# A triangular inverse by levels: the products of levels 1 to 4 on diagonal blocks of 32 instead of 64

## The chip, the cores and the metric

The kernel runs on one core of a Trainium2 chip. The metric is the device time of one execution in microseconds, as the median of several executions. One execution was also recorded by the hardware profiler; its rows are what this document argues from.

## The reference

The program is a stack of two models over 256 tokens of width 1024 in float32, with feed-forward blocks, several token mixers and norms. Two of its mixers are gated delta rules with 8 heads of width 128, worked in chunks of 64 tokens. For each chunk and head a lower triangular system is solved:

```python
CHUNK = 64
GDN_HEADS = 8

def gated_delta_rule(q, k, v, g, beta):
    ...
    a_mat = jnp.where(strict, jnp.einsum('nbhid,nbhjd->nbhij', kb, kc) * decay, 0.0)
    t_mat = a_mat + jnp.eye(CHUNK, dtype=jnp.float32)
    rhs = jnp.concatenate([vc * bc[..., None], kb * jnp.exp(gc)[..., None]], axis=-1)
    sol = lax.linalg.triangular_solve(t_mat, rhs, left_side=True, lower=True, unit_diagonal=True)
    value, kcd = sol[..., :dv], sol[..., dv:]
    ...
```

The matrix `t_mat` is 64x64, with ones on its diagonal. There are 4 chunks and 8 heads in each mixer, 32 such systems.

## The kernel before

The kernel writes out the program of each engine by hand, and semaphores connect them. All weights come through one stream of chunks of 1 MB: SyncE loads a chunk, ACT makes its rounded part `w_hi` (`split_high`, L395), DVE the rest `w_lo` (`split_low`, L402), and PE multiplies with three matmuls for each pair of 128x128 tiles (L408 to L410). A gated-delta mixer goes through its input chunks in steps `u`. In step `u` PE runs `before(u)`, the first half of the product with chunk `u`, `middle(u)`, and the second half. The small products of the delta rule are put in `before` and `middle`.

The kernel inverts the triangular matrices instead of solving. A pair of chunks is held at once, one on partitions 0 to 63 and one on 64 to 127; `t` (0 or 1) counts the pairs, and `h` the 8 heads. `g_A` holds the matrix below the diagonal, `g_T` and `g_TT` the inverse so far and its transpose. Level 0 makes the inverses of the 2x2 blocks on the diagonal, and level `v` joins blocks of 2^v rows into blocks of 2^(v+1), up to level 5, which joins two of 32 (`LEVELS` is 6). A level takes three products and two steps on DVE:

- `right(v)` on PE (in `middle`): the product of `g_A` and `g_T` into PSUM bank `4 + t`. DVE multiplies it by the mask of the level into `g_Y` (`right_set`, L2904); the mask has ones in only those entries that this level fills.
- `both(v)` on PE (in `before` of the next step): `g_TT` with `g_Y` into bank `4 + t` (not at level 5), and `g_Y` with `g_TT` into bank `6 + t`. DVE subtracts whole banks from `g_T` (L2910) and from `g_TT` (L2911), in `inverse_set`.

Each product is made by `blocks`, whose 16 matmuls are 64 rows by 64 columns on the two diagonal 64x64 tiles of the array:

```python
        def blocks(bank, lhs, rhs):

            for h in range(HN):
                for r in CK:
                    last = nc.tensor.matmul(ps[r, bank, CHUNK * h:CHUNK * h + CHUNK], lhs[r, h, :], rhs(r, h), start=True, stop=True)
            return last
```

All these operands are float32 and not its rounded form, and a matmul of theirs is two records of weight load and two of matmul in the trace. `right(1)` is in `middle(10)`, `both(1)` in `before(11)`, and so on to `right(5)` in `middle(14)` and `both(5)` in `before(15)`. Between them DVE also works on the convolution (L2844), the scaled values (L2921) and `w_lo`.

Of the kernel before, what the change touches and what calls it, by code (L numbers as in the profile page):

```python
# [24 lines left out]
CHUNK = 64  # L25
# [157 lines left out]
LEVELS = 6  # L183
# [63 lines left out]
def two_block_model(nc, w, out):  # L247

    plan, start = weight_plan(w)
# [34 lines left out]
    ps = ctx.enter_context(nc.psum_tensor("ps", [P, 8, 512], F32))  # L284
# [546 lines left out]
    def cols(k, a, b, rows=slice(0, P)):  # L831
        return ws[k][rows, a:b]
# [21 lines left out]
    blocks = cols(5, 800, 1760).rearrange("p (v j n) -> p v j n", v=2, n=2 * N_CMP)  # L854
# [840 lines left out]
    HN = 8  # L1695
# [97 lines left out]
    def mixer_tensor(pe, i, xpass_out, edge):  # L1793
        (gdn_tensor, mlstm_tensor, diff_tensor)[i % 3](pe, i, xpass_out, edge)
# [521 lines left out]
    def by_block(k, part):  # L2316
        return ws[k][:, D * part:D * part + D].rearrange("p (t h c) -> p t h c", t=TT, c=CHUNK)

    def chunk_tmp(e):
        return ws[9][:, D + 512 * (e % 2):D + 512 * (e % 2) + 512].rearrange("p (a s) -> p a s", a=2)  # L2320
# [3 lines left out]
    g_dec, g_A, g_T, g_TT, g_Y = by_block(6, 0), by_block(6, 1), by_block(7, 0), by_block(7, 1), by_block(9, 0)  # L2324
# [33 lines left out]
    inv_y, inv_ys, inv_z, inv_t = (gp("inverse_right", TT * LEVELS), gp("inverse_right_set", TT * (LEVELS - 1)),  # L2358
                                   gp("inverse_both", TT * (LEVELS - 1)), gp("inverse_set", TT * LEVELS))
# [56 lines left out]
    def gdn_tensor(pe, i, xpass, edge):  # L2416
# [4 lines left out]
# [6 lines that stand above are left out]
# [43 lines left out]
        def turned_chunk(bank, src):  # L2470

            for t in range(TT):
                for a in range(2):
                    last = nc.tensor.transpose(ps[:, bank, (2 * t + a) * P:(2 * t + a + 1) * P], src[:, a, t * P:(t + 1) * P], ident)
            last.then_inc(gd_tn.sem, 1)
# [6 lines left out]
        def v_turned(c):  # L2482
# [4 lines left out]
                done(gd_ssx, 0)  # L2487
            turned_chunk(3, chunk_tmp(c))

        def right(v):  # L2490
            for t in range(TT):
                if v == 1:
                    done(gd_T0, t)
                else:
                    done(inv_t, TT * (v - 1) + t)
                blocks(4 + t, g_A[:, t, :, :], lambda r, h: g_T[r, t, h, :]).then_inc(inv_y.sem, 1)

        def both(v):
            for t in range(TT):
                done(inv_ys, TT * (v - 1) + t)  # L2500
                if v < LEVELS - 1:
                    blocks(4 + t, g_TT[:, t, :, :], lambda r, h: g_Y[r, t, h, :])
                blocks(6 + t, g_Y[:, t, :, :], lambda r, h: g_TT[r, t, h, :]).then_inc(inv_z.sem, 1)

        def values_reads(t):
            done(inv_t, TT * (LEVELS - 1) + t)
# [59 lines left out]
        def before(u):  # L2566
# [24 lines left out]
            if 11 <= u <= 15:  # L2591
                both(u - 10)
# [8 lines left out]
        def middle(u):  # L2601
            if u == 8:
                for t in range(TT):
                    if t == 0:
                        done(gd_kc, 1)
                    token_products(4 + t, g_kT, g_kT, t).then_inc(gd_kk.sem, 1)
            if 10 <= u <= 14:
                right(u - 9)
            if u == 15:
                values_reads(0)  # L2610
            if u == 16:
                done(gd_z, 2)
                attention(1)
                first_gain()
# [8 lines left out]
        for u in range(3, 17):  # L2623
# [5 lines left out]
            bank = (u - 1) % 3  # L2629
# [596 lines left out]
```

## Time and profile before

| what | value |
|---|---|
| median of 3 runs | 2469.0 us (2468.1 to 2474.7) |
| the profiled execution | 2470.6 us |
| its span, first to last instruction | 2468.8 us |
| PE, matmuls | 2403.3 us busy, 97% of the span |
| PEld, weight loads | 2222.7 us, 90% |
| DVE | 1501.5 us, 61% |
| ACT | 1068.1 us, 43% |
| POOL | 151.8 us, 6% |
| granted TensorE clock, mean | 0.993 |

PE is the matmul side of TensorE and PEld its weight loads, which overlap. The ends of matmuls are modelled, and records overlap, so the busy time of a group is the time that its records cover together, and the spacing of their starts says more than the length of one. A shape `64*64 64x128` is 64 rows by 64 weight columns, with 64 rows of 128 moving columns.

### The profile page before, as it was taken

How to read it: one execution, taken by the hardware profiler on the slowest of the kernel's cores; microseconds unless marked ns; L12 is line 12 of the kernel's file. 1: busy time of each engine (PE TensorE's matmuls, PEld its weight loads, DVE VectorE, ACT ScalarE, POOL GpSimd, SP SyncE). 2: the span in 40 equal slices, each digit the busy share in tenths (PEclk: the TensorE clock that was granted, in tenths of full speed). 3: DMA queues.
4: the chain of work that ended last, by engine and by line, in shares of the span. 5: the costliest groups of instructions: out<-in, count | busy, mean ns of one | idle time of the engine just before them, and what ended most of it. 6: DMA issues, size and time to landing. Idle time of an engine off the chain costs nothing. (4 is left out here: it accounts for less than half of the span.)

```text
span 2468.8 us, 42893 instructions
## 1 busy us (share of the span) xinstructions
PE 2403.3 (97%) x18882; PEld 2222.7 (90%) x18882; DVE 1501.5 (61%) x2042; ACT 1068.1 (43%) x1319; POOL 151.8 (6%) x177
## 2 busy tenths in 40 slices
PE   8999999999999999999999999999998999999998
PEld 8999889999999799899889989899997998998997
DVE  5457664465567645667565556755676556866554
ACT  4334643333336543363343345533465335533432
POOL 0100000020000100001110000100001000111000
PEclk9999999999999999999999999999999999999999
DMA  6756355575564455543155554555545555423553
GB/s 228 241 188 155 107 175 184 186 226 190 185 165 128 151 187 186 158 139 104 53 196 188 188 156 137 171 188 188 178 137 171 188 188 162 121 87 103 181 188 118
DMA packets 320809, 405.37 MB, mean 164 GB/s; under 512 B 48688, under 2 KB 281232, under 8 KB 320624
## 3 DMA queue, kind: packets, MB, share of 16 engines
q1 hardware_dynamic: 314960, 383.50, 49.1%
q0 software_dynamic: 5664, 19.13, 2.5%
q8 instruction: 149, 2.44, 0.4%
q14 instruction: 36, 0.29, 0.0%
HBM read 401.55 MB, written 1.05 MB: 163 GB/s over the span
## 5 line engine op out<-in xcount | busy, mean ns | idle before, releaser
L402 DVE TENSOR_TENSOR w_lo<-raw,w_hi 128x2048 fp32r<-128x2048 f32 (+2 forms) x363 | 813.6, 2266 | 123.7 <-ACT w_hi L395 123.4
L395 ACT CAST w_hi<-raw 128x2048 fp32r<-128x2048 f32 (+2 forms) x363 | 685.5, 1890 | 462.5 <-PE ps L410 403.8
L408 PE MATMUL ps<-aT_hi,w_hi 128*128 128x256 f32 x2840 | 810.3, 285 | 0.0
L409 PE MATMUL ps<-aT_lo,w_hi 128*128 128x256 f32 x2840 | 804.4, 283 | 0.0
L410 PE MATMUL ps<-aT_hi,w_lo 128*128 128x256 f32 x2840 | 804.3, 283 | 0.0
L408 PEld LDWEIGHTS ps<-aT_hi,w_hi 128*128 128x128 f32 x2840 | 543.3, 191 | 7.0 <-issue 1.9
L409 PEld LDWEIGHTS ps<-aT_lo,w_hi 128*128 128x128 f32 x2840 | 543.5, 191 | 4.2 <-issue 0.5
L410 PEld LDWEIGHTS ps<-aT_hi,w_lo 128*128 128x128 f32 x2840 | 543.3, 191 | 0.5
L408 PE MATMUL ps<-w_hi,h_hi 128*128 128x512 f32 x928 | 363.6, 392 | 5.8 <-DVE h_lo L1758 4.6
L409 PE MATMUL ps<-w_lo,h_hi 128*128 128x512 f32 x928 | 362.6, 391 | 0.0
L410 PE MATMUL ps<-w_hi,h_lo 128*128 128x512 f32 x928 | 361.4, 389 | 0.0
L408 PE MATMUL ps<-w_hi,aT_hi 128*128 128x256 f32 (+2 forms) x992 | 303.7, 306 | 18.0 <-DVE aT_lo L732 14.4
L409 PE MATMUL ps<-w_lo,aT_hi 128*128 128x256 f32 (+2 forms) x992 | 297.1, 299 | 0.0
L410 PE MATMUL ps<-w_hi,aT_lo 128*128 128x256 f32 (+2 forms) x992 | 297.0, 299 | 0.0
L408 PEld LDWEIGHTS ps<-w_hi,aT_hi 128*128 128x128 f32 x992 | 191.6, 193 | 29.2 <-DVE aT_lo L732 17.5
L408 PEld LDWEIGHTS ps<-w_hi,h_hi 128*128 128x128 f32 x928 | 174.8, 188 | 40.8 <-DVE h_lo L1758 6.0
L410 PEld LDWEIGHTS ps<-w_hi,h_lo 128*128 128x128 f32 x928 | 174.5, 188 | 37.1
L409 PEld LDWEIGHTS ps<-w_lo,h_hi 128*128 128x128 f32 x928 | 174.9, 188 | 32.6
L593 DVE TENSOR_TENSOR ws<-ws 128x512 f32<-128x512 f32 x64 | 44.2, 691 | 262.1 <-ACT ws L686 262.1
L410 PEld LDWEIGHTS ps<-w_hi,aT_lo 128*128 128x128 f32 x992 | 191.8, 193 | 5.8
L409 PEld LDWEIGHTS ps<-w_lo,aT_hi 128*128 128x128 f32 x992 | 191.9, 193 | 5.2
L593 DVE TENSOR_TENSOR ws<-ws,ps 128x512 f32<-128x512 f32 x44 | 30.2, 687 | 258.4 <-PE ps L410 258.4
(370 smaller groups left out, 1944.6 us busy)
## 6 DMA issues: line engine op xcount, KB each, us to landing
raw<-in_mlp_w SPq DMA_DIRECT2D x128, 1024.0 KB, 5.4
raw<-in_ffn_wd SPq DMA_DIRECT2D x44, 1024.0 KB, 4.9
raw<-in_ffn_wg SPq DMA_DIRECT2D x43, 1024.0 KB, 5.3
raw<-in_ffn_wu SPq DMA_DIRECT2D x43, 1024.0 KB, 5.3
raw<-in_gdn_w_in SPq DMA_DIRECT2D x32, 1024.0 KB, 5.7
raw<-in_mlstm_w_in SPq DMA_DIRECT2D x12, 1024.0 KB, 5.4
raw<-in_diff_w_in SPq DMA_DIRECT2D x12, 1024.0 KB, 5.3
raw<-in_w_in SPq DMA_DIRECT2D x8, 1024.0 KB, 5.2
```

Of the source, the lines that this page charges most:

```text
L395: nc.scalar.copy(used_part(hi_slot(n), n), used_part(raw[:, n % RAW, :], n)).then_inc(hi_ready, 1)
L402: nc.vector.tensor_tensor(used_part(lo_slot(n), n), used_part(raw[:, n % RAW, :], n), used_part(hi_slot(n), n).bitcast(F32), ALU.subtract) ...
L408: nc.tensor.matmul(dst, l_hi, r_hi, start=start, stop=False)
L409: nc.tensor.matmul(dst, l_hi, r_lo, start=False, stop=False)
L410: return nc.tensor.matmul(dst, l_lo, r_hi, start=False, stop=stop)
L593: nc.vector.tensor_tensor(hidden_buffer(s), gate, up, ALU.mult).then_inc(hid_made, 1)
```

## The change

A new function `blocks_of_32` makes a product for the levels 1 to 4: for each head, four matmuls of 32 rows and 32 weight columns, one on each of the four diagonal 32x32 tiles of the array, which `tile_position` names. Everything off these diagonal blocks is left out. At these levels the mask has no entry there, and `g_T` and `g_TT` are zero there. Since DVE still subtracts whole banks, the bank must hold zeros off the blocks: in `both(1)` the product into bank `6 + t` therefore takes all 64 moving columns (`zeros_too`), and the later levels leave these entries as they are. Bank `4 + t` holds zeros there since the product with the identity in `before(10)`, which `blocks` still makes whole. Level 5 and all work on DVE and ACT stay as they were.

```diff
--- before.py
+++ after.py
@@ -2487,20 +2487,37 @@
                 done(gd_ssx, 0)
             turned_chunk(3, chunk_tmp(c))
 
+        def blocks_of_32(bank, lhs, rhs, zeros_too=False):
+
+            for h in range(HN):
+                for q in range(4):
+                    r, own = slice(32 * q, 32 * q + 32), slice(32 * (q % 2), 32 * (q % 2) + 32)
+                    c = slice(0, CHUNK) if zeros_too else own
+                    last = nc.tensor.matmul(ps[r, bank, CHUNK * h + c.start:CHUNK * h + c.stop], lhs[r, h, own], rhs[r, h, c],
+                                            start=True, stop=True, tile_position=(32 * q, 32 * q))
+            return last
+
         def right(v):
             for t in range(TT):
                 if v == 1:
                     done(gd_T0, t)
                 else:
                     done(inv_t, TT * (v - 1) + t)
-                blocks(4 + t, g_A[:, t, :, :], lambda r, h: g_T[r, t, h, :]).then_inc(inv_y.sem, 1)
+                if v < LEVELS - 1:
+                    last = blocks_of_32(4 + t, g_A[:, t, :, :], g_T[:, t, :, :])
+                else:
+                    last = blocks(4 + t, g_A[:, t, :, :], lambda r, h: g_T[r, t, h, :])
+                last.then_inc(inv_y.sem, 1)
 
         def both(v):
             for t in range(TT):
                 done(inv_ys, TT * (v - 1) + t)
                 if v < LEVELS - 1:
-                    blocks(4 + t, g_TT[:, t, :, :], lambda r, h: g_Y[r, t, h, :])
-                blocks(6 + t, g_Y[:, t, :, :], lambda r, h: g_TT[r, t, h, :]).then_inc(inv_z.sem, 1)
+                    blocks_of_32(4 + t, g_TT[:, t, :, :], g_Y[:, t, :, :])
+                    last = blocks_of_32(6 + t, g_Y[:, t, :, :], g_TT[:, t, :, :], v == 1)
+                else:
+                    last = blocks(6 + t, g_Y[:, t, :, :], lambda r, h: g_TT[r, t, h, :])
+                last.then_inc(inv_z.sem, 1)
 
         def values_reads(t):
             done(inv_t, TT * (LEVELS - 1) + t)
```

What PE now has in place is seen from the order of its instructions in the built program; `x64` is the count of equal matmuls one after the other. First, the start of step 11 in the first mixer, where `before(11)` stands between the product of chunk 10 and that of chunk 11. Before:

```order
L408 MATMUL ps<-aT_hi,w_hi 128x256
L409 MATMUL ps<-aT_lo,w_hi 128x256
L410 MATMUL ps<-aT_hi,w_lo 128x256
L2425 MATMUL ps<-ws 64x64 x64
L2474 MATMUL ps<-consts,ws 128x128 x4
L408 MATMUL ps<-aT_hi,w_hi 128x256
L409 MATMUL ps<-aT_lo,w_hi 128x256
L410 MATMUL ps<-aT_hi,w_lo 128x256
```

and with the change:

```order
L408 MATMUL ps<-aT_hi,w_hi 128x256
L409 MATMUL ps<-aT_lo,w_hi 128x256
L410 MATMUL ps<-aT_hi,w_lo 128x256
L2496 MATMUL ps<-ws 32x32 x32
L2496 MATMUL ps<-ws 32x64 x32
L2496 MATMUL ps<-ws 32x32 x32
L2496 MATMUL ps<-ws 32x64 x32
L2474 MATMUL ps<-consts,ws 128x128 x4
L408 MATMUL ps<-aT_hi,w_hi 128x256
L409 MATMUL ps<-aT_lo,w_hi 128x256
L410 MATMUL ps<-aT_hi,w_lo 128x256
```

The 64 matmuls of `both(1)` are now 128, the half of them with 64 moving columns. They stand in the same place, ahead of the four transposes of L2474. The two pairs of rows are the two values of `t`.

Second, the middle of the same step, where `right(2)` stands between the two halves of the product. Before:

```order
L408 MATMUL ps<-aT_hi,w_hi 128x256
L409 MATMUL ps<-aT_lo,w_hi 128x256
L410 MATMUL ps<-aT_hi,w_lo 128x256
L2425 MATMUL ps<-ws 64x64 x32
L408 MATMUL ps<-aT_hi,w_hi 128x256
L409 MATMUL ps<-aT_lo,w_hi 128x256
L410 MATMUL ps<-aT_hi,w_lo 128x256
```

and with the change:

```order
L408 MATMUL ps<-aT_hi,w_hi 128x256
L409 MATMUL ps<-aT_lo,w_hi 128x256
L410 MATMUL ps<-aT_hi,w_lo 128x256
L2496 MATMUL ps<-ws 32x32 x64
L408 MATMUL ps<-aT_hi,w_hi 128x256
L409 MATMUL ps<-aT_lo,w_hi 128x256
L410 MATMUL ps<-aT_hi,w_lo 128x256
```

The 32 matmuls of `right(2)` are 64, and nothing around them moved. The orders on DVE, ACT, POOL and SP have no row more or less than before.

## Rows read from the trace of the kernel before

**Rows 1.** The page: its first line and part 1.

```profile
span 2468.8 us, 42893 instructions
...
PE 2403.3 (97%) x18882; PEld 2222.7 (90%) x18882; DVE 1501.5 (61%) x2042; ACT 1068.1 (43%) x1319; POOL 151.8 (6%) x177
...
```

**Rows 2.** Stretches between starts of products: busy us (count) by engine.

```profile
...
core 0: us, PE busy (x) PEld busy (x) DVE busy (x) ACT busy (x) POOL busy (x), PEclk, DMA share, GB/s
1117.72:1128.27 10.55, 10.55 (x181) 10.15 (x181) 10.24 (x14) 4.62 (x7) 2.58 (x2) 1.00 0.37 103
1128.27:1140.68 12.41, 12.41 (x245) 12.01 (x244) 10.72 (x15) 3.26 (x4) 3.20 (x1) 1.00 0.30 87
1140.68:1153.10 12.42, 12.42 (x246) 12.02 (x245) 9.28 (x14) 3.89 (x5) 1.28 (x1) 1.00 0.31 87
...
```

**Rows 3.** Timeline of PE there: start us, length us, what, records.

```profile
...
1123.19 2.08 PE L2425 MATMUL ps<-ws 64*64 64x64 f32 x64
...
1128.27 3.95 PE L2425 MATMUL ps<-ws 64*64 64x64 f32 x128
1132.15 0.66 PE L2474 MATMUL ps<-consts,ws 128*128 128x128 f32 x4
...
1140.68 3.95 PE L2425 MATMUL ps<-ws 64*64 64x64 f32 x128
...
```

**Rows 4.** PE groups by shape: records | busy us, mean ns of one | idle.

```profile
...
L2425 PE MATMUL ps<-ws 64*64 64x64 f32 x1792 | 56.6, 219 | 0.0
...
L2548 PE MATMUL ps<-ws 128*64 128x128 f32 x96 | 12.1, 277 | 0.6 <-DVE ws L2950 0.6
...
L2523 PE MATMUL ps<-ws 64*128 64x64 f32 x128 | 8.0, 275 | 0.0
...
L2562 PE MATMUL ps<-ws 64*64 64x128 f32 x128 | 7.9, 272 | 0.0
...
L992 PE MATMUL ps<-ws 128*64 128x30 f32 x128 | 4.1, 222 | 0.0
L1025 PE MATMUL ps<-ws 128*128 128x64 f32 x32 | 4.0, 278 | 0.0
...
```

**Rows 5.** Timeline of PE, two shapes with 128 moving columns.

```profile
...
1208.49 1.91 PE L2556 MATMUL ps<-ws 128*64 128x128 f32 x16
...
1212.31 1.96 PE L2562 MATMUL ps<-ws 64*64 64x128 f32 x32
...
```

**Rows 6.** Weight loads in flight between 1140.68 and 1140.70 us.

```profile
...
1140.68 0.14 PEld L2425 LDWEIGHTS ps<-ws 64*64 64x64 f32 x2
```

**Rows 7.** Timeline of DVE through one step, releaser in brackets.

```profile
...
1142.81 0.69 DVE L2910 TENSOR_TENSOR ws<-ws,ps 128x512 f32<-128x512 f32 x1 [2.19 <-PE ps L2425]
...
1144.68 0.69 DVE L2910 TENSOR_TENSOR ws<-ws,ps 128x512 f32<-128x512 f32 x1 [0.58 <-PE ps L2425]
...
1145.88 2.68 DVE L2844 SCALAR_TENSOR_TENSOR ws<-ps,small,ws 128x255 f32<-128x255 f32 x6
...
1149.21 0.69 DVE L2904 TENSOR_TENSOR ws<-ps,gb 128x512 f32<-128x512 f32 x1
1150.15 0.69 DVE L2904 TENSOR_TENSOR ws<-ps,gb 128x512 f32<-128x512 f32 x1 [0.24 <-PE ps L2425]
1150.76 2.28 DVE L402 TENSOR_TENSOR w_lo<-raw,w_hi 128x2048 fp32r<-128x2048 f32 x1
1155.23 0.69 DVE L2910 TENSOR_TENSOR ws<-ws,ps 128x512 f32<-128x512 f32 x1 [2.19 <-PE ps L2425]
...
```

**Rows 8.** Waits of 1100 to 1215 us: total us, times, longest.

```profile
...
DVE ws L2910 <- PE ps L2425: 9.6, 8, 2.2
...
```

## The prediction

> **What bounds the kernel now.** The first line and part 1 of the page come first: PE is busy for 2403.3 us of a span of 2468.8 us, 97%, and DVE for 61% [rows 1]. With so little idle time on PE, a change is worth what it takes from or adds to PE's own work, as long as no other engine becomes late. The change touches only the triangular inverse in the two gated-delta mixers, so the second view is the table of stretches, cut at the starts of the products of both(v) in the first of those mixers. Each stretch is one step: PE is busy in all of it (12.42 of 12.42 us), at a granted clock of 1.00 (the level of 2.4 GHz), and DVE for 9.28 us of a 12.42 us step, 10.72 us of the one before [rows 2]. The third view, the timeline of PE, shows where the inverse stands in a step: 128 records of line 2425 in a row for both(v), 3.95 us, and 64 for right(v), 2.08 us [rows 3]. In the waits, it is DVE that waits for these products (9.6 us in all, 8 times) and not PE for DVE [rows 8]. So the inverse is PE work on the path that sets the end, from first to last.
>
> **What a product costs now.** A program matmul of float32 operands appears as two records: both(v) has 64 of them and the row shows x128. A record is 218 ns long, but the rows of 3.95 and 2.08 us give (3.95 - 0.22) / 127 = 29.4 ns and (2.08 - 0.22) / 63 = 29.5 ns from start to start [rows 3, 4]. Two things make up these 29.4 ns. First, two tiles of the array work at once: within the first 20 ns of a both(v) two weight loads are in flight, and both are over after 0.14 us [rows 6]. The same shows over whole groups: 96 records with 128 moving columns on one tile are busy for 12.1 us (126 ns each), 128 records on two alternating tiles for 7.9 us (62 ns each); with 128 weight columns and 64 moving ones it is 4.0 us for 32 on one tile and 8.0 us for 128 on two [rows 4]. I call one record on each tile a round: now 2 x 29.4 = 58.7 ns. Second, the length of a round follows the wider of the two sides, weight columns or moving columns. With 64 and 128, L2562 takes (1.96 - 0.27) / 31 x 2 = 109 ns per round [rows 5]; with 64 and 30, L992 costs as much per record (4.1 us for 128) as the 64 and 64 of L2425 (56.6 us for 1792) [rows 4]. From 128 to 64 a round falls from 109 to 58.7 ns, by 50.
>
> **The change part by part.** For the levels 1 to 4 each 64x64 product becomes two of 32x32, on four diagonal tiles instead of two. Per mixer, right(1) to right(4) had 4 x 32 matmuls and both(1) to both(4) had 4 x 64: 384, that is 768 records in 384 rounds of two. After it there are 768 matmuls, 1536 records, in 384 rounds of four, if four tiles work at once. Both sides are then 32 wide. No row of the trace has a product of 32 columns on four tiles, so its round is bounded from both sides. From above in cost: a record takes what it takes today, 29.4 ns, whatever its size, and a round of four costs 118 ns. From below: width halved once more takes half of the 50 ns, 25, from the 58.7 ns, which gives 33 ns; a round proportional to width would give 29 ns, not far from it. I take 33 ns, since both a single-tile and a two-tile row show the halving, and nothing in them shows records on different tiles waiting for each other. One group stays wide: in both(1) the second product writes the zeros too, with 64 moving columns, so its 32 rounds stay at about 58.7 ns.
>
> The sum: 384 - 32 = 352 rounds per mixer, 25.7 ns less each, is 9.05 us; two mixers make **18.1 us**. The edges of a group (the change to another tile size and back) are there before and after alike, 16 groups each; I cost them at nothing more. Everything that follows in a mixer moves ahead by 9 us: PE is busy before and after it, and the DMA share in these steps is 0.30 to 0.37, so loads aren't late [rows 2]. DVE and ACT have the same instructions, each over the whole 64 columns, so they get neither more nor less.
>
> DVE must keep up with a shorter step. Now it starts on L2910 2.13 us after both(v) begins (1142.81 - 1140.68), 1.88 us of which is the first half of the products [rows 3, 7]. With 32 rounds of 33 ns that becomes 1.06 + 0.25 = 1.3 us. Then follow, by their starts, two pairs of updates (1.20 us each, 1144.68 to 1145.88), six taps of the convolution and the scaled values (1145.88 to 1149.21, 3.33 us), two masks (1.3 us without the 0.24 us wait) and the split (2.28 us) [rows 7]: 1.3 + 2.4 + 3.3 + 1.3 + 2.3 = 10.6 us. A step of PE shrinks by 96 rounds x 25.7 ns = 2.5 us to 9.95 us, and its next first half is ready at 9.95 + 1.3 = 11.25 us. DVE is 0.6 us early, where today it waits 2.19 us; PE needs the masks at 9.95 us and has them at 8.3 us. The cover holds, but it is thin in the step of 10.72 us. If it were gone, PE would wait for what is missing, some tenths of a us in a step.
>
> Predicted: 2469.0 - 18.1 = 2450.9, rounded **2451 us** in the median; the profiled execution of before took 2470.6 us around its span of 2468.8, 1.6 us above the median, so a profile of after should have a span near 2451 too.
>
> The Trainium skill says, in TensorE: Matmul & The Clock Gate, Part 3, under The mechanism, that matmuls on different tile positions run concurrently, starting about 4 ns apart. The trace agrees for two tiles, by the two loads within 20 ns; no run here shows it for four. A rule that speaks against the change stands in TensorEngine Tiling (Array Packing), Instruction Overhead: each matmul has some 60 cycles of overhead, so a small dimension should not be cut further. The first page puts this floor at about 25 ns from start to start; if it held across tiles, an estimate from it would be 1536 x 25 - 768 x 29.4 = 15.8 us more per mixer, and the kernel would take 2501 us. The first rival below is this case as the rows can price it. If the floor held for each tile alone, it would change nothing in my sum. The L992 row agrees with a floor of either kind or with none.
>
> **The rivals.**
> *Records are the cost (slower).* What feeds the array hands out one record each 29.4 ns, and the tiles only seem to set it. For it: 30 and 64 moving columns cost the same, 32 and 31.6 ns, and no group in the rows lies under that. Against it: two loads start within 20 ns of each other and then none for most of a round, so records do come in quick pairs. Price: 768 more records per mixer x 29.4 ns = 22.6 us, 45 us in all, 2514 us. It decides from 29.4 / 2 = 14.7 ns per record on; above that the kernel gets slower. Chance with milder forms of it (2480 to 2514 us): 0.18.
> *Only two tiles at a time (within 0.3%, at its edge).* The second record of a float32 matmul must follow the first on the same tile, and if records start strictly in order, a third tile waits behind it. Then a pair of records costs a round of 33 ns: 704 pairs x 33 less 352 x 58.7 is 2.6 us per mixer, and the wide product of both(1) doubles to 64 x 58.7, 1.9 us more: 4.5 us per mixer, 9 us, 2478 us; with a round of 29 ns, 2472 us. Against it: nothing in the two-tile rows; no row has more tiles. Chance, with all that nearly cancels: 0.12.
> *DVE takes over, or four tiles don't fill (faster, but less).* If DVE's chain is 1 us longer than I added up, or a round is 40 to 45 ns, 6 to 13 us are left: 2456 to 2463 us. For it: the DVE load of 10.72 us in the step with both(1). Chance: 0.10.
> *The forecast*, 2447 to 2455 us: 0.60.
>
> **How the numbers follow.** A measurement of this kernel can tell about 0.3%, 7.4 us, from no change. Faster by more than that takes the forecast and the third rival: 0.70. The second gives 0.10 of its 0.12 to no change and the rest to slower: 0.10 and 0.20. The range from 2446 us (a round of 29 ns gives 2469.0 - 704 x 29.7 ns = 2448, and 2 us for the spread) to 2478 us, the end of the second rival, leaves out only the first one, 0.18. The forecast's own range is 2447 to 2455 us.
>
> **What the profile of after would show.** Right: L2496 in place of most of L2425, 3072 records with a start each 8 ns; a right(v) row of 128 records about 1.2 us long instead of 2.08, a both(v) row of 256 about 2.3 us; steps of about 10 us where there were 12.42; the wait of L2910 for PE down from 2.2 us to under 1 us, and none of PE for DVE. Wrong, first rival: a both(v) of 7.5 us and steps of 18 us. Wrong, second: right(v) as long as now. Wrong, third: idle time of PE before L2496, released by L2904 or L2911. The forecast fails on the one term that no row shows, the round of four tiles.

## The result and the profile after

The changed kernel takes 2500.0 us in the median (2498.1 to 2500.3), the kernel before 2469.7 us in the same comparison: a ratio of 1.012 with an interval of 1.0108 to 1.0132, slower by about 30 us. The prediction was 2451 us with a range up to 2478 us. Its sign was wrong.

First line and part 1 of the page of the changed kernel:

```profile
span 2497.8 us, 45965 instructions
...
PE 2403.6 (96%) x20418; PEld 2223.0 (89%) x20418; DVE 1502.1 (60%) x2042; ACT 1068.2 (43%) x1319; POOL 152.3 (6%) x177
```

PE is busy for as long as before (2403.3 us, [rows 1]) in a span that is 29 us longer. What is added to the span is time in which PE stands still. (That its busy time is the same doesn't say that its work is; see the parts of the loss below.) The groups by shape (records | busy us, mean ns | idle us ahead of them) say where; L2496 is the matmul of the new function, L2927 is what [rows 7] calls L2910:

```profile
L2496 PE MATMUL ps<-ws 32*32 32x32 f32 x2816 | 30.7, 196 | 25.4 <-issue 25.4
L2425 PE MATMUL ps<-ws 64*64 64x64 f32 x256 | 8.3, 220 | 0.0
L2496 PE MATMUL ps<-ws 32*32 32x64 f32 x256 | 5.3, 238 | 0.0
```

25.4 us of idle time stand ahead of L2496 and are put down to "issue": the profile shows no semaphore, no engine and no transfer of data that was waited for. The waits of PE have two more places of that kind (line waited at <- what: us in total, times, longest); L408 has its 1.0 us in kernels without the change as well:

```profile
PE ps L2496 <- issue: 25.4, 9, 4.8
PE ps L2467 <- issue: 2.3, 1, 2.3
PE ps L2474 <- issue: 1.7, 1, 1.7
PE ps L408 <- issue: 1.0, 1, 1.0
```

That is 29.4 us of stalls. The timeline of PE in the first gated-delta mixer (start us, length us, what, records, idle time before) shows that right(v) is what the prediction said, and that both(v) is not:

```profile
1121.93 1.31 PE L2496 MATMUL ps<-ws 32*32 32x32 f32 x128
...
1126.23 1.99 PE L2496 MATMUL ps<-ws 32*32 32x32 f32 x166
1129.98 1.30 PE L2496 MATMUL ps<-ws 32*32 32x32 f32 x90 [1.76 <-issue]
...
1134.67 1.31 PE L2496 MATMUL ps<-ws 32*32 32x32 f32 x128
...
1138.97 1.15 PE L2496 MATMUL ps<-ws 32*32 32x32 f32 x113
1140.64 1.30 PE L2496 MATMUL ps<-ws 32*32 32x32 f32 x128 [0.52 <-issue]
1146.58 0.43 PE L2496 MATMUL ps<-ws 32*32 32x32 f32 x15 [4.64 <-issue]
...
1156.01 1.81 PE L2496 MATMUL ps<-ws 32*32 32x32 f32 x188
1162.03 1.17 PE L2496 MATMUL ps<-ws 32*32 32x32 f32 x68 [4.20 <-issue]
```

right(v) takes 1.31 us for 128 records where it took 2.08 us for 64 [rows 3]: (1.31 - 0.20) / 127 = 8.7 ns from start to start, a round of four in 35 ns, against the forecast of 33. The first both(v) (1126.23) is broken once, the next one (1138.97) twice, and lasts 8.0 us from first to last where 3.95 us stood [rows 3]. Between the two breaks at 1140.64 and 1146.58 lie exactly 128 records. Stretches cut at the ends of the breaks count the others:

```profile
core 0: us, PE busy (x) PEld busy (x) DVE busy (x) ACT busy (x) POOL busy (x), PEclk, DMA share, GB/s
1129.90:1140.60 10.70, 10.14 (x383) 9.64 (x383) 7.80 (x12) 2.15 (x4) 0.32 (x1) 1.00 0.17 53
1140.60:1146.50 5.90, 1.30 (x128) 1.20 (x128) 1.28 (x2) 1.11 (x1) 0.00 (x0) 0.70 0.55 167
1146.50:1162.00 15.50, 11.24 (x383) 10.76 (x383) 9.19 (x14) 3.89 (x5) 1.27 (x1) 0.83 0.21 71
```

A record is a weight load and a matmul, two instructions. 128 records are 256 instructions; 383 records with the two semaphore waits between them are 768, three times 256. Every break lies at a multiple of 256 instructions from the others: counted through the trace, that is so for all 11 breaks that make the 29.4 us, and for all 71 in the traces of the runs below. The 1.0 us at L408 isn't such a break. Part 3 of the page has a queue that carries instructions (queue, kind: packets, MB, share):

```profile
q1 hardware_dynamic: 314960, 383.50, 48.7%
q0 software_dynamic: 5664, 19.13, 2.5%
q8 instruction: 161, 2.64, 0.4%
```

2.64 MB in 161 packets are 16.4 KB each, or 64 bytes for each of 256 instructions. The same row of the kernel before:

```profile
q8 instruction: 149, 2.44, 0.4%
```

The 12 packets more fit the 1536 more records, 3072 instructions. The DMA view of two neighbouring stretches ahead of the break of 4.64 us shows what the packet did; first 1140.0 to 1144.1 us, then 1144.1 to 1146.5 us:

```profile
DMA packets 1026, 1.04 MB, mean 253 GB/s; under 512 B 12, under 2 KB 1026, under 8 KB 1026
...
q1 hardware_dynamic: 1026, 1.04, 86.1%
...
DMA packets 15, 0.03 MB, mean 11 GB/s; under 512 B 4, under 2 KB 14, under 8 KB 14
...
q8 instruction: 1, 0.02, 2.7%
q1 hardware_dynamic: 14, 0.01, 1.3%
```

In the first only the 1 MB of weights moves. The packet of instructions runs in the second, as that load ends: it starts at 1144.17, and PE goes on at 1146.58. In all 82 breaks PE goes on 2.2 to 2.9 us after the last packet of that queue started. What follows a long break is slow as well (stretches; the granted clock is the third column from the end):

```profile
core 0: us, PE busy (x) PEld busy (x) DVE busy (x) ACT busy (x) POOL busy (x), PEclk, DMA share, GB/s
1130.00:1136.00 6.00, 6.00 (x247) 5.73 (x246) 4.58 (x10) 0.63 (x1) 0.22 (x1) 1.00 0.21 72
...
1143.00:1150.00 7.00, 3.42 (x30) 3.35 (x30) 2.89 (x6) 0.00 (x0) 0.00 (x0) 0.51 0.16 54
1160.00:1170.00 10.00, 7.97 (x100) 7.91 (x99) 3.81 (x8) 1.26 (x2) 1.28 (x1) 0.50 0.05 17
...
1134.67:1151.71 17.04, 11.88 (x438) 11.31 (x437) 10.24 (x17) 3.94 (x6) 0.00 (x0) 0.80 0.22 64
1151.71:1170.25 18.54, 14.34 (x442) 13.76 (x441) 8.59 (x13) 4.46 (x6) 2.56 (x2) 0.73 0.18 60
```

The last two rows are whole steps, from one right(v) to the next: 17.0 and 18.5 us for the 12.4 us of [rows 2]. The clock is 1.00 before the longer breaks, and 0.50 (1.2 GHz) around and after the long ones. Over the whole span the mean granted clock is 0.984 where it was 0.993. With half clock as the only other level that is 2497.8 x 0.016 x 2 = 80 us at 1.2 GHz, against 2468.8 x 0.007 x 2 = 35 us: 45 us more.

### The profile page after: what moved, and what is told of

It is laid out like the page before. It is cut to its first block and busy times, and to the rows that moved or that the text cites. A ratio compares the mean times of both kernels' runs of the same rounds, so it can differ in the third digit from the quotient of the medians.

```text
span 2497.8 us, 45965 instructions
## 1 busy us (share of the span) xinstructions
PE 2403.6 (96%) x20418; PEld 2223.0 (89%) x20418; DVE 1502.1 (60%) x2042; ACT 1068.2 (43%) x1319; POOL 152.3 (6%) x177
## 3 DMA queue, kind: packets, MB, share of 16 engines
q8 instruction: 161, 2.64, 0.4%
## 5 line engine op out<-in xcount | busy, mean ns | idle before, releaser
L408 PE MATMUL ps<-aT_hi,w_hi 128*128 128x256 f32 x2840 | 816.5, 288 | 0.0
L410 PE MATMUL ps<-aT_hi,w_lo 128*128 128x256 f32 x2840 | 809.8, 285 | 0.0
L408 PEld LDWEIGHTS ps<-aT_hi,w_hi 128*128 128x128 f32 x2840 | 549.5, 193 | 8.8 <-issue 3.9
L409 PEld LDWEIGHTS ps<-aT_lo,w_hi 128*128 128x128 f32 x2840 | 549.6, 194 | 4.2 <-issue 0.5
L410 PEld LDWEIGHTS ps<-aT_hi,w_lo 128*128 128x128 f32 x2840 | 549.2, 193 | 0.5
L408 PE MATMUL ps<-w_hi,h_hi 128*128 128x512 f32 x928 | 363.6, 392 | 5.5 <-DVE h_lo L1758 4.2
L410 PE MATMUL ps<-w_hi,h_lo 128*128 128x512 f32 x928 | 361.3, 389 | 0.0
L408 PE MATMUL ps<-w_hi,aT_hi 128*128 128x256 f32 (+2 forms) x992 | 303.0, 305 | 18.0 <-DVE aT_lo L732 14.4
L410 PE MATMUL ps<-w_hi,aT_lo 128*128 128x256 f32 (+2 forms) x992 | 296.2, 299 | 0.0
L408 PEld LDWEIGHTS ps<-w_hi,aT_hi 128*128 128x128 f32 x992 | 191.6, 193 | 28.7 <-DVE aT_lo L732 17.4
L408 PEld LDWEIGHTS ps<-w_hi,h_hi 128*128 128x128 f32 x928 | 174.8, 188 | 40.6 <-DVE h_lo L1758 5.7
L410 PEld LDWEIGHTS ps<-w_hi,h_lo 128*128 128x128 f32 x928 | 174.4, 188 | 37.0
L410 PEld LDWEIGHTS ps<-w_hi,aT_lo 128*128 128x128 f32 x992 | 191.4, 193 | 5.5
```

Of the source, the lines that this page charges most:

```text
L408: nc.tensor.matmul(dst, l_hi, r_hi, start=start, stop=False)
L409: nc.tensor.matmul(dst, l_hi, r_lo, start=False, stop=False)
L410: return nc.tensor.matmul(dst, l_lo, r_hi, start=False, stop=stop)
```

## The experiments

All times are medians; "before" is the kernel before on the same chip in the same comparison.

**1. right(v) alone.** both(v) keeps its blocks of 64.

```
-                if v < LEVELS - 1:
-                    blocks_of_32(4 + t, g_TT[:, t, :, :], g_Y[:, t, :, :])
-                    last = blocks_of_32(6 + t, g_Y[:, t, :, :], g_TT[:, t, :, :], v == 1)
+                if v < LEVELS - 1:
+                    blocks(4 + t, g_TT[:, t, :, :], lambda r, h: g_Y[r, t, h, :])
+                last = blocks(6 + t, g_Y[:, t, :, :], lambda r, h: g_TT[r, t, h, :])
```

> Only right(1) to right(4) are made of 32x32 blocks; both(v) stays as before. Theory A (PE's instructions come in blocks of 256, and a block takes some 3.4 us to be there): a step then has 616 PE instructions in about 11.6 us instead of 872, a burst of 256 at most, so nothing stalls; each right(v) takes 1.24 us instead of 2.01, eight of them save 6.2 us: 2463 us, idle time of PE on issue before L2496 under 2 us. Theory B (four tiles at once make PE stall now and then, in proportion to their records): the kernel after lost about 48 us on 3072 such records (30 us more time and 18 us of forecast gain), 1024 records lose 16 us and save 6: 2479 us.

2463.0 us, before 2468.8: ratio 0.9976 (0.9966 to 0.9986), 5.8 us faster. Eight rows shorter by 0.77 us make 6.2 us. No stall in either mixer. So a round of four tiles is worth what it was forecast to be.

**2. both(v) alone.** The other way about: right(v) by blocks of 64, both(v) by blocks of 32. The banks that right(v) fills are then not zero off the blocks, so these entries of the inverse differ; the work is otherwise that of the change.

```
-                if v < LEVELS - 1:
-                    last = blocks_of_32(4 + t, g_A[:, t, :, :], g_T[:, t, :, :])
-                else:
-                    last = blocks(4 + t, g_A[:, t, :, :], lambda r, h: g_T[r, t, h, :])
+                last = blocks(4 + t, g_A[:, t, :, :], lambda r, h: g_T[r, t, h, :])
```

> Only both(1) to both(4) are made of 32x32 blocks; right(v) stays as before. Theory A: each both(v) is still a burst of 512 instructions in little more than 2 us, so at least one whole block of 256 lies in it and PE stalls 2.3 us or more each time, 8 times, and the clock falls after the longer ones: 2487 to 2502 us, nearly all of the loss of the kernel after. Theory B: 2048 of the 3072 records: 32 us lost and 12 us saved, 2490 us. It says which part the loss sits in, not which theory holds.

2505.3 us, before 2468.8: ratio 1.0147 (1.0133 to 1.0161), 3 us over theory A's range and 15 over B's figure. The loss belongs to both(v) and needs no right(v). The timeline of PE has one stall a step, 4.35, 5.00 and 4.46 us in the first three. From one to the next it lies 11 records later in both(v), so a step is three blocks less 22 instructions, 746, and has the same boundary in each burst:

```profile
1123.19 2.75 PE L2496 MATMUL ps<-ws 32*32 32x32 f32 x230
1130.29 1.01 PE L2496 MATMUL ps<-ws 32*32 32x64 f32 x26 [4.35 <-issue]
...
1141.36 2.25 PE L2496 MATMUL ps<-ws 32*32 32x32 f32 x241
1148.61 0.44 PE L2496 MATMUL ps<-ws 32*32 32x32 f32 x15 [5.00 <-issue]
```

**3. Half of the heads.** Every second head is left out of all products by blocks of 32, so half of that work is missing.

```
-            for h in range(HN):
+            for h in range(0, HN, 2):
```

> The 32x32 products are made for four of the eight heads only, so the inverses of the others are wrong. PE then has as many instructions in a step as the kernel before (384 + 104), all on four tiles. Theory A: 488 instructions in a step of about 8 us need two blocks, no stall or nearly none (under 3 us in all); both(v) about 1.2 us, right(v) about 0.65 us, so 2469.7 - 32 = 2438 us (2436 to 2444). Theory B: half of the records, half of the loss: 24 us of stalls and slow clock less 32 us of work left out, 2460 us.

2444.3 us, before 2468.8: ratio 0.9906 (0.989 to 0.9921). The stalls nearly vanish (1.3 us ahead of L2496, twice, and 0.7 us more at L408 than in the kernel before) with half of the new instructions, while tiles, shapes and order are those of the change. What costs is how many instructions there are, not that a product has four tiles. It is 6 us over the 2438 us named, though the profiled execution took 2441.5 us: even here a few stalls remain.

**4. One of both(v)'s two products.**

```
                 if v < LEVELS - 1:
                     blocks_of_32(4 + t, g_TT[:, t, :, :], g_Y[:, t, :, :])
-                    last = blocks_of_32(6 + t, g_Y[:, t, :, :], g_TT[:, t, :, :], v == 1)
-                else:
-                    last = blocks(6 + t, g_Y[:, t, :, :], lambda r, h: g_TT[r, t, h, :])
+                last = blocks(6 + t, g_Y[:, t, :, :], lambda r, h: g_TT[r, t, h, :])
```

> right(v) and the product of both(v) that goes into bank 4 + t are made of 32x32 blocks, the one into bank 6 + t of 64x64. Theory A: 744 instructions in a step of about 10.8 us, where 2.9 blocks of 3.4 us take 9.9: the average is supplied, but a both(v) is 384 instructions in 3 us, so a block that lies whole in it costs up to 1.4 us. 2469.7 - 12.8 = 2457 us without stalls, up to 2467 with them. Theory B: 2048 records lose 32 us and save 12.8: 2489 us.

2484.0 us, before 2468.8: ratio 1.0055 (1.0042 to 1.0068). That is 17 us over theory A's range and 5 us under B's 2489, so by the time alone B was the better one. PE stalls by 16.4 us in all (here and below without the 1.0 us at L408), up to 3.4 us at a time, now also within rows of L2425, which the change leaves alone. All its breaks lie at multiples of 256 instructions, so the mechanism stands, but my count of it had no room for a packet that comes late. That led to runs 6 and 7.

**5. The blocks moved.** One product of 64 records is made twice, ahead of both(1).

```
                     done(inv_t, t)
+                    blocks(4 + t, g_TT[:, t, :, :], lambda r, h: id64[r, :])
                     blocks(4 + t, g_TT[:, t, :, :], lambda r, h: id64[r, :]).then_inc(inv_y.sem, 1)
```

> The changed kernel with 64 more records (128 instructions) per mixer ahead of both(1): the product with the unit matrix is made twice. Theory A (TensorE's instructions come in blocks of 256, and it stands still at a block's edge when the next block has not come): the stalls of the first delta-net mixer lie 64 records earlier in the work than in the changed kernel, so the first one in both(1) comes after record 102 of both(1) instead of 166, and the one in both(2) after record 49 instead of 113; in the second such mixer, shifted by 2 x 64 records = one whole block, they lie where they lay in the changed kernel. Theory B (the stalls belong to what is computed there: a bank, a tile, a semaphore of VectorE): they stay after records 166 and 113 in both mixers. Time 2495 to 2506 us by both.

2506.8 us (two runs; before 2468.9), 1 us over the range. The stall in both(1) comes after record 230 and the one in both(2) after record 177, against 166 and 113 in the changed kernel; in both(3) after 124 against 188. All three moved by 64 records, modulo the 128 of a block: my 102 and 49 were the boundary one block earlier, at which the next block was there in time. In the second mixer, moved by a whole block, the first stall is back after record 185, as in the changed kernel. Theory B is out: the same matmul stalls or not by its place in the stream.

```profile
1127.59 2.75 PE L2496 MATMUL ps<-ws 32*32 32x32 f32 x230
1134.14 1.01 PE L2496 MATMUL ps<-ws 32*32 32x64 f32 x26 [3.80 <-issue]
...
1144.59 1.71 PE L2496 MATMUL ps<-ws 32*32 32x32 f32 x177
1150.35 1.29 PE L2496 MATMUL ps<-ws 32*32 32x32 f32 x79 [4.05 <-issue]
...
1161.33 1.25 PE L2496 MATMUL ps<-ws 32*32 32x32 f32 x124
1163.89 1.30 PE L2496 MATMUL ps<-ws 32*32 32x32 f32 x128 [1.31 <-issue]
```

**6. Weight loads after both(v).** The changed kernel, with one wait more on SyncE.

```
         for n in range(start["in", i], start["out", i] + 4):
+            u = n - RAW - start["in", i]
+            if i % 3 == 0 and 10 <= u <= 14:
+                sp.wait_ge(inv_z.sem, inv_z.count(i // 3, TT * (u - 9) - 1))
             load_chunk(sp, n)
```

> The changed kernel, same instructions of TensorE in the same order; only the weight loads that began about 1 us after both(v) began now begin when both(v) is done (SyncE waits for the product's semaphore). Theory A (the fetch of a block of 256 instructions waits behind the 1 MB weight load that runs then, 5.5 to 6.4 us a block instead of 3.4): the stalls of 4.2 to 4.6 us shrink to 0.5 to 2 us, fewer stretches at half clock, 2472 to 2486 us. Theory C (the load has no part in it): the stalls stay and the time is 2497 to 2503 us; later weights that themselves delay the products would show as PE waits on the split of the weights, and more time.

2487.3 us, before 2468.9: ratio 1.0079 (1.0063 to 1.0094), 12.7 us less than the changed kernel, with the same instructions on TensorE. The same 128 records that stood between two breaks at 1140.64 and 1146.58, 5.94 us, are here 3.74 us apart:

```profile
1137.92 1.15 PE L2499 MATMUL ps<-ws 32*32 32x32 f32 x113
1139.52 1.30 PE L2499 MATMUL ps<-ws 32*32 32x32 f32 x128 [0.44 <-issue]
1143.26 0.32 PE L2499 MATMUL ps<-ws 32*32 32x32 f32 x15 [2.45 <-issue]
```

So a block needs some 3.5 us even with the DMA engines free (3.3 us is the least that lies between two packets in the traces of runs 4, 6 and 9 and of the changed kernel), and 5.9 us here behind a weight load. Most of the stalls that remain are of 1.5 to 2.5 us, more than the 0.5 to 2 us expected, and put the time 1 us over theory A's range.

**7. The same with one of the two products.** The edits of 4 and 6 together.

> The kernel with right(v) and one of both's two products by blocks of 32 (2484 us), with the weight loads begun only when both(v) is done. Theory A: 744 instructions a step of 12.4 us are 2.9 blocks of 3.4 us = 9.9 us, so with no load in the way the stalls go nearly: 2457 to 2466 us. Theory C (the load has no part in it): 2480 to 2487 us.

2470.6 us, before 2468.9: ratio 1.0009 (0.9999 to 1.002), 13.4 us less than run 4, and 5 us over A's range. The stalls fell from 16.4 to 5.7 us.

**8. Cut in halves as well.** Run 7's kernel; the second half of both(v) and of right(v) each come some matmuls later, between features of the convolution's input, which are the matmuls of L408 to L410 in these steps.

```
+                if early is not None and (ft, k) in early:
+                    early[ft, k]()
...
+                    early[0, 3] = lambda: both(u - 10, (1,))
...
+                    early[1, 2] = lambda: right(u - 9, (1,))
```

> The kernel with right(v) and one of both's two products by blocks of 32 and with later weight loads (2470.6 us), with both(v) and right(v) cut in their halves: t = 1 of both(v) comes three inner steps (nine records, 1.1 us) into the features product, t = 1 of right(v) two inner steps into its second half. Theory A (supply of instructions by blocks of 256, 3.4 us each): 744 instructions a step in four bursts of at most 384 leave hardly a stall; the array work saved against right(v) alone is half of what both(v) saves, about 6 us, of which some is given back at whatever stalls are left: 2456 to 2463 us, at or under the kernel with right(v) alone (2463 us). Rival: what is left above 2463 us in the kernel with later loads is no stall but something that the 32-blocks of both(v) cost in themselves: 2467 to 2472 us.

2464.5 us, before 2469.2: ratio 0.998 (0.9971 to 0.9989). Beside the 1.0 us at L408, which the control has too, no stall is left; the time is between the two expectations. The steps are no shorter than with right(v) alone, where rows of both(v) start 11.65 us apart:

```profile
1121.45:1133.23 11.78, 11.78 (x374) 10.94 (x373) 9.13 (x12) 2.83 (x4) 5.78 (x2) 1.00 0.07 14
1133.23:1145.19 11.96, 11.95 (x373) 11.02 (x372) 9.08 (x15) 3.26 (x4) 0.00 (x0) 1.00 0.30 92
```

The edges say why. The timeline of PE in run 4, where both forms alternate:

```profile
1124.03 0.75 PE L2496 MATMUL ps<-ws 32*32 32x32 f32 x64
1124.72 1.15 PE L2425 MATMUL ps<-ws 64*64 64x64 f32 x32
1125.80 0.75 PE L2496 MATMUL ps<-ws 32*32 32x32 f32 x64
```

The product by blocks of 32 is 0.69 us from start to start. The one by blocks of 64 is 1.08 us there, where 32 x 29.4 ns = 0.94 us: the change between forms costs 0.14 us. So a product saves 0.94 - 0.69 - 0.14 = 0.11 us, 0.22 us a step, and two cuts with an edge of about 0.2 us each give it back (around right(v), the two gaps to the neighbouring features are 0.21 and 0.22 us where two features are 0.12 us apart).

**9. The whole change, later loads, both(v) in halves.** The edits of 6 and of 8, the latter for both(v) alone and with two inner steps between.

> The changed kernel with the later weight loads, and both(v) cut in its two halves: t = 1 comes after the first six records of the features product that followed both(v) (about 0.8 us), so that the same instructions come less densely. Theory A (density of instructions against the supply): less than the kernel with later loads alone, by 0 to 8 us: 2468 to 2482 us. Rival: VectorE gets the second half's result 0.8 us later, and right(v + 1) waits for it: 5 us and more above the kernel with later loads alone, with PE idle ahead of right(v + 1) released by VectorE.

2475.3 us, before 2468.9: ratio 1.0028 (1.0018 to 1.0038), 12 us less than run 6, where 0 to 8 us were named, and inside theory A's range, with issue stalls of 12.8 us in place of 21. PE did not wait for VectorE before right(v). Same instructions, same products, 25 us less than the changed kernel, by when the instructions fall due and what the DMA engines do then.

**10. Control.** The kernel before with the edit of 6 alone.

> Control: the kernel before, with the weight loads of these steps begun only when both(v) is done, and nothing else. Theory A, by which later loads only help a fetch that is short of time: no stalls here to help, 2466 to 2472 us. If the later loads gain or lose something by themselves (the splits of the weights come later and PE waits on them, or the other way about), it shows here, and the numbers of the kernels with later loads are to be read less that amount.

2468.8 us, before 2469.2: ratio 1.0002 (0.9993 to 1.0011). Later loads do nothing by themselves that can be told from noise.

**11. As many instructions on two tiles.** Run 1's kernel, each matmul of both(v) cut in two of 32 columns.

```
+            for h in range(HN):
+                for r in CK:
+                    for c in (0, 32):
+                        last = nc.tensor.matmul(ps[r, bank, CHUNK * h + c:CHUNK * h + c + 32], lhs[r, h, :], rhs[r, h, c:c + 32],
+                                                start=True, stop=True)
```

> right(v) by blocks of 32, both(v) by whole blocks of 64 rows as before but each matmul cut in two of 32 columns: as many instructions as the changed kernel has (both(v) 512 instead of 256), on two tiles as before, the same results. Theory A (it is the number of instructions in the time, not the tiling): idle time put down to issue comes back in the features and both stretches at blocks of 256, 0.5 to 2.5 us a step, though less than in the changed kernel since these records take longer: 2475 to 2500 us, with stretches at half clock. Rival B (the tiles of 32 rows bring the stalls): no issue stalls; 2463 us plus whatever the added records take in the array, 0 to 16 us, all of it seen as a longer both(v) without idle time.

2506.7 us, before 2469.2: ratio 1.0152 (1.0138 to 1.0166), above both expectations, for a reason of its own. The timeline of PE:

```profile
1124.36 7.92 PE L2505 MATMUL ps<-ws 64*64 64x32 f32 x256
...
1155.82 5.78 PE L2505 MATMUL ps<-ws 64*64 64x32 f32 x188
1162.43 3.94 PE L2505 MATMUL ps<-ws 64*64 64x32 f32 x68 [0.83 <-issue]
```

A record with 32 moving columns takes (7.92 - 0.22) / 255 = 30.2 ns, as long as one with 64: with 64 weight columns the weight side sets the round, so both(v) doubles, 8 x 4.0 = 32 us. With the 3.6 us of stalls that makes 2463.0 + 32 + 3.6 = 2499 us; the other 8 us go with a lower mean clock (0.989, run 1 has 0.994). This slows the stream itself, and the run can't say what dense records on two tiles would do. What it does show: the stalls that are left (3.6 us) come, among others, after record 188 of both(3), and after 185 of both(1) in the second mixer, the same places as in the changed kernel, in products that have no tile of 32 rows.

**12. right(v) whole, both(v) in halves.** Run 8 without its second entry.

> The kernel of the last look but with right(v) whole again: right(v) and one of both's two products by blocks of 32, later weight loads, and only both(v) cut in its halves, the second three inner steps (nine records) into the features product. In the kernel with right(v) cut as well (2464.5 us) no stall was left, but its step took 11.8 to 12.1 us, about as long as with right(v) alone (11.65 us), since each cut adds an edge between forms of some 0.2 us. Theory A (edges, not stalls, are what is left): eight edges fewer, 1.6 us, if no stall comes back: 2461 to 2464 us. Rival: right(v) whole (256 instructions at once) brings a stall of 0.5 to 1 us back in some steps: 2464 to 2468 us, with idle time put down to issue.

2465.0 us (2457.4 to 2469.5), before 2469.1: ratio 0.9978 (0.9969 to 0.9988). Stalls of 0.2 us, under the 0.5 us of the rival, in whose range the time lies. It can't be told from run 8, so the eight edges fewer are not shown in the time. No version that does the whole work has a median under that of right(v) alone, 2463.0 us, though runs 8 and 12 can't be told from it.

## Why the prediction was wrong

- **The round of four tiles** was the term that I called the one that could fail. It held: 35 ns for 33, and run 1 brought 5.8 us of the 6.2 us that its rows make. Without stalls the whole change would have saved 6.2 us in right(v). both(v) would be 256 x 8.7 ns = 2.2 us at the levels 2 to 4, and at level 1, where the records with 64 columns are some 14 ns apart, 2.9 us, in place of the 3.88 us to the next start [rows 3]: 2 x (3 x 1.65 + 0.97) = 11.8 us. Together 18.0 us, against a forecast of 18.1.
- **The step that failed** is the sum's "352 rounds ... 25.7 ns less each". It prices a product by its rounds in the array and takes the supply of instructions as free. Twice the records in less time are 872 instructions of PE a step instead of 488. At the 3.5 us that a block of 256 needs, 872 / 256 x 3.5 = 11.9 us a step, for a step that I had put at 9.95 us; and both(v), 512 instructions in 2.3 us, needs two blocks in the time of less than one. The term left out measured 30.2 + 18.0 = 48.2 us.
- **Its parts.** 29.4 us are the stalls themselves. The remaining 18.8 us are mostly the half clock. Added up from the trace's clock records, it is 0.50 for 81.6 us here and for 33.9 us in the kernel before, 47.7 us more, of which 10.4 us pass in stalls. Two matmuls of L408 to L410 start 213 ns apart at 0.50 and 120 ns apart at 1.00 (medians). An estimate from these numbers: (213 - 120) / 213 of the other 37.3 us, 16.3 us. That is nearly what the smaller tiles save, and why PE's busy time is the same as before: 2403.3 - 18.0 + 16.3 = 2401.6 us, where 2403.6 was measured. That the stalls cause the fall is likely, not shown. Both go together in run 6 (21 us of stalls, mean clock 0.988), run 9 (12.8 us, 0.992) and run 8 (none, 0.993), but run 4 has 16.4 us at 0.992, and run 11 only 3.6 us at 0.989.
- **"The DMA share in these steps is 0.30 to 0.37, so loads aren't late"** was true of the loads and missed who else uses the engines. In the kernel before, the same weight load starts 1 us after both(v) does, and packets of instructions come at its end just as well (at 1133.41 and 1145.70 us in the trace, with loads that end at 1133.44 and 1145.98); PE stood still for none of them, and two packets are never under 4.49 us apart there. By runs 6 and 10, 12.7 us of the change's time are this collision, and nothing without the change.
- **The rivals.** "Records are the cost" had the direction and the wrong mechanism: it said 29.4 ns a record everywhere, a both(v) of 7.5 us and steps of 18 us. A both(v) of 8.0 us and steps of 17 and 18.5 us did appear, but right(v) stayed at 8.7 ns a record, which the rival excludes. The Trainium skill's floor of about 25 ns from start to start (TensorE: Matmul & The Clock Gate, Part 2, Back-to-back issue gap) does not hold across four tiles by these rows. That the estimate from it, 2501 us, met the time was chance.
- **DVE's cover** held: no wait of PE for the masks or the updates (`right_set`, `inverse_set`), even in run 9 with its result later. It is DVE that waits for PE in the stalls.

The Trainium skill describes this supply in Runtime: NRT & Kernel Launch, Instruction fetch mechanics: blocks of 16 KiB, 256 instructions, each fetched over a DMA queue while the one before runs. The packets and the distances of 256 agree. It also says that the fetch is hidden, because instructions are issued more slowly than it fills. Here issue ran at about 4.4 ns an instruction in right(v) against 3.5 us / 256 = 14 ns of supply, and it was not hidden. The page gives TensorE's buffer 2048 instructions, eight blocks. The traces show only one ready ahead. If the last packet before a break carries the block behind it, and the others follow in order, then in none of the 14 traces does a packet start more than 1.16 blocks (some 300 instructions) before the first instruction of its block: the next one is fetched only when PE is about to enter the one before it. That is also where the 3.5 us come from. After the end of a break the next packet starts 1.04 us later at the earliest, and PE goes on at least 2.2 us after that, so two blocks can't follow each other in less than some 3.3 us.

**Open:** what passes in the 1 us before a packet starts, and in the rest of the 2.2 to 2.9 us, when the packet itself is over in about 1 us; what makes the clock fall, since no run held clock and stalls apart; and what the 2.5 us are that the estimate leaves, edges of shapes perhaps.

## What to carry to other kernels

Count instructions, not only array time. Before a matmul is cut into smaller tiles, divide the instructions of the engine in the busiest few microseconds by 256 and set them against some 3.5 us a block, more where a large transfer starts at the same time. If idle time put down to "issue" recurs at distances of 128 records, spread the burst and keep big loads out of it (25 us here), or cut only the products that stay under the supply: right(v) alone beat the kernel before by 0.2% and the changed one by 1.5%. Its burst of 256 instructions ran through on the one block in reserve, where both(v)'s 512 did not.

## What the runs showed of the hardware that was not expected

- Records of float32 products start 8.7 ns apart on four diagonal tiles of 32x32 (1.31 us for 128), against 29.4 ns on two of 64x64: 3.4 times as many records in a time, not twice.
- With 64 weight columns a record with 32 moving columns costs what one with 64 does (30.2 and 29.4 ns).
- PE's instructions arrive in packets of 256. PE stands still for up to 5.0 us when one is late, and the packet of a burst waited until a 1 MB load had ended: 3.74 us between the ends of two breaks without the load, 5.94 us with it, for the same 128 records.
- Stretches at 1.2 GHz come with the stops, but their length does not follow the stop's. In the changed kernel 6.8 and 10.2 us go with stops of 4.64 and 4.20 us; in run 2 a stop of 5.00 us is followed by 3.4 us, and in run 11 one of 0.83 us, in a dense row of small matmuls, by 10 us. In all, 48.2 us were lost where 29.4 us of stops stand.
- No packet of instructions starts before PE is about to enter the block ahead of the one it carries, so at most one block waits in reserve (14 traces).
